# One layer of a hybrid decoder with 32 experts on one core: the scatter of the 64-row tile on quarters of the array, expert weights in 2 MB transfers of 16 KB pieces, waits at every second chunk

## The chip, the cores and the metric

The kernel runs on one core of one Trainium2 chip (trn2). The metric is the device time of one execution in microseconds; lower is better. "PE" in the profile is TensorE, "PEld" its loads of the array's stationary operand, "DVE" VectorE, "ACT" ScalarE, "POOL" GpSimd and "SP" SyncE, which issues all DMAs here.

## What is computed

One step of a decoder layer for 320 tokens (256 of a prompt, 64 of eight short sequences), all in float32: a norm, one input projection, two kinds of recurrent mixers, an output projection, then a mixture of experts, a gated embedding and a last norm. The change is almost wholly in the experts. Their part of the reference, cut:

```python
logits = (xt @ router_w + router_b)                 # 320 x 32
top_val, top_idx = lax.top_k(logits, 4)
gates = jax.nn.softmax(top_val, axis=-1)
# the tokens of each expert in blocks of rows; for each block:
hgu = xb @ w_gu[e] + b_gu[e]                        # w_gu: 32 x 1024 x 2048
gate = jnp.minimum(hgu[:, :D_FF], 7.0)
up = jnp.clip(hgu[:, D_FF:], -7.0, 7.0)
act = (up + 1.0) * gate * jax.nn.sigmoid(1.702 * gate)
y = act @ w_down[e] + b_down[e]                     # w_down: 32 x 1024 x 1024
# gate * y is added to the rows of its tokens
```

## The kernel before

All 32 experts are run, each on a block of up to 64 token slots, and each expert's weights (8 MB for gate and up, 4 MB for down) pass through SBUF once. `ring` is a buffer of 12 slots of 1 MB (8 KB in each of 128 partitions); chunk `c` of an expert stands in slot `c`: eight up chunks (`NGU`), then four down chunks. SyncE loads a chunk with one DMA (L254) as soon as the semaphore `w_used` says that the slot's last reader is through, and the DMA's landing raises `w_full{c}`, on which TensorE waits before the chunk's first matmul. In SyncE's loop (L366 to L376) stand eight waits and loads of gate-up chunks for the next expert and four of down chunks for this one.

TensorE's order is written out by hand in `expert(b, age)` (L1102). A pass of the loop does, for block `b`:

- eight times `up_chunk` (L1074): each chunk has four matmuls, two pairs. A pair uses the two halves of the array's columns: 64 token slots are the stationary operand, the gate columns of the weights stream through the one half and the up columns through the other, 512 columns at a time.
- between them, for block `b - 2`, three times `scatter` (L1064), behind chunks 1, 2 and 3: the expert's result `yS` (64 slots; output columns 0 to 511 in partitions 0 to 63, columns 512 to 1023 in partitions 64 to 127) is multiplied by the transposed selection `SELT`, once for each tile of tokens. Tiles 0 and 1 have 128 tokens, tile 2 has 64. The two matmuls of a scatter use the two halves of the array's rows and write banks 5 and 6 of PSUM. VectorE then adds the banks to `X` (L1976, two adds of 512 columns), and the next scatter waits for that (semaphore `x2`).
- behind chunk 4 `gather(b + 1)` (L1038): the next block's rows are picked out of `XS` by six matmuls; ScalarE copies them to `xrow` (L1362). Behind chunk 6 `turn_rows` (L1046): four transposes of them; ScalarE copies the outcome to `xg` (L1366).
- `turn_select(b - 1)` (L1054): three transposes of the gated selection.
- `down(b - 1)`: four `down_chunk` (L1084), each with four matmuls.
- `turn_hidden(b)` (L1094): eight transposes of the hidden rows `hS`, which ScalarE has copied from PSUM (L1370, L1371). VectorE (L1984 and after) and ScalarE make `act_t` of them, while TensorE goes on.

Which rows of the weights lie in a partition decides which columns must be transposed together. A down chunk holds two neighbouring rows of `w_down` in each partition (`(j p i)`, `i=2`), 8 KB in one piece, and so `turn_hidden` reads every second column of `hS`. Each piece of a gate-up chunk is one row of `w_gu`, 8 KB, and `turn_rows` reads `xrow` column by column:

```python
w_gu = a["expert_w_gu"].rearrange("o e (k p) n -> (o e) p k n", p=P)
w_dn = a["expert_w_down"].rearrange("o e (j p i) n -> (o e) p j (i n)", p=P, i=2)
...
def pair_cols(m):
    return slice(2 * P * (m // 2) + m % 2, 2 * P * (m // 2 + 1), 2)
```

The gate-up bias is transposed once at the start in the same order of columns (L524), sixteen transposes. Blocks 0 and 1 stand ahead of the loop, which runs 30 times; behind it the last down chunks are loaded to slots 0 to 3 and the last sums are made (L1136, L1143), then the gated embedding follows (L1173, L1191).

## Time and profile before

| what | value |
|---|---|
| median of 3 runs | 1428.64 us (1428.08 to 1430.69) |
| profiled execution | 1428.37 us |
| its span, first to last instruction | 1426.6 us |
| TensorE busy | 1343.8 us |
| loads of the array busy | 582.8 us |
| VectorE, ScalarE busy | 503.7, 202.4 us |
| read from HBM | 433.41 MB |
| mean rate over the span | 307 GB/s |
| mean granted clock of TensorE | 0.964 of full speed |

A row of the groups (rows 5 below) gives the line, the engine, what is written and read, the size of the operand, the count, then busy time and mean duration of one, then the idle time ahead of it and what ended it. One matmul of the program appears as two records in the trace, and so does its load; a transpose appears as one. A row of the chain (rows 2, 7 and 8) gives the start, the length and the engine and line that the end of the program hangs on at that time; it follows starts and ends of whole groups, so a piece holds what its group takes including the change to the next.

### The profile page before, as it was taken

How to read it: one execution, taken by the hardware profiler on the slowest of the kernel's cores; microseconds unless marked ns; L12 is line 12 of the kernel's file. 1: busy time of each engine (PE TensorE's matmuls, PEld its weight loads, DVE VectorE, ACT ScalarE, POOL GpSimd, SP SyncE). 2: the span in 40 equal slices, each digit the busy share in tenths (PEclk: the TensorE clock that was granted, in tenths of full speed). 3: DMA queues.
4: the chain of work that ended last, by engine and by line, in shares of the span. 5: the costliest groups of instructions: out<-in, count | busy, mean ns of one | idle time of the engine just before them, and what ended most of it. 6: DMA issues, size and time to landing. Idle time of an engine off the chain costs nothing.

```text
span 1426.6 us, 17293 instructions
## 1 busy us (share of the span) xinstructions
PE 1343.8 (94%) x6116; PEld 582.8 (41%) x6116; DVE 503.7 (35%) x1073; ACT 202.4 (14%) x385; POOL 53.8 (4%) x103
## 2 busy tenths in 40 slices
PE   6989997798669999999999999999999999999997
PEld 5755686573433333333333333333333333333332
DVE  2583344735316233222332223322233222322233
ACT  2450000000111111111111111111111111111111
POOL 5100001000200000000000000000000000000000
PEclk9999999977679999999999999999999999999999
DMA  8231103111459999999999999999999999999931
GB/s 258 68 115 59 59 1 136 58 59 48 120 215 376 421 422 422 422 422 422 422 422 422 422 422 421 422 422 422 420 422 422 422 422 422 422 422 422 422 149 37
DMA packets 83620, 438.82 MB, mean 308 GB/s; under 512 B 15114, under 2 KB 22423, under 8 KB 34410
## 3 DMA queue, kind: packets, MB, share of 16 engines
q1 hardware_dynamic: 83594, 438.47, 75.7%
q8 instruction: 17, 0.28, 0.1%
q14 instruction: 9, 0.07, 0.0%
HBM read 433.41 MB, written 5.02 MB: 307 GB/s over the span
## 4 chain that ended last, share of the span: by engine, by line
PE 89%; DVE 6%; ACT 1%; issue 1%; DMA 1%; SPq 1%; POOLq 0%; POOL 0%; ACTq 0%; DVEq 0%
PE bank L1074 32%; PE bank L1084 16%; PE bank L1064 7%; PE bank L1038 6%; PE bank L576 6%; PE bank L1094 3%; PE bank L1173 2%; PE bank L744 2%; PE bank L574 1%; PE bank L1046 1%; DVE SC L1506 1%; PE bank L1054 1%; PE bank L1014 1%; PE bank L787 1%; DMA SC<-in_ple_w 1%
## 5 line engine op out<-in xcount | busy, mean ns | idle before, releaser
L1074 PE MATMUL bank<-ring,SC 128*64 128x512 f32 x2048 | 479.1, 600 | 0.7 <-ACT SC L1366 0.7
L1074 PEld LDWEIGHTS bank<-ring,SC 128*64 128x64 f32 x2048 | 133.2, 136 | 282.2 <-issue 277.5
L1084 PE MATMUL bank<-ring,SC 128*64 128x512 f32 x1024 | 226.8, 595 | 0.0
L1984 DVE TENSOR_TENSOR SC<-bank,bgu 128x256 f32<-128x256 f32 x128 | 48.1, 418 | 437.1 <-PE bank L1094 437.1
L1976 DVE TENSOR_TENSOR X<-X,bank 128x512 f32<-128x512 f32 x180 | 115.1, 679 | 97.2 <-PE bank L1064 97.2
L1084 PEld LDWEIGHTS bank<-ring,SC 128*64 128x64 f32 x1024 | 70.7, 137 | 133.3 <-issue 133.3
L576 PE MATMUL bank<-xT,ring 128*128 128x320 f32 x384 | 112.5, 442 | 5.8 <-ACTq L1265 4.3
L1064 PE MATMUL bank<-SC 64*128 64x512 f32 x360 | 101.6, 641 | 0.0
L1038 PE MATMUL bank<-XS,SC 128*64 128x512 f32 x396 | 90.6, 592 | 0.7 <-ACT va L1352 0.7
L576 PEld LDWEIGHTS bank<-xT,ring 128*128 128x128 f32 x384 | 71.5, 193 | 36.2 <-ACTq L1265 6.9
L1362 ACT ACTIVATE SC<-bank 128x512 f32<-128x512 f32 x33 | 19.7, 597 | 407.0 <-PE bank L1038 407.0
L1960 DVE TENSOR_SCALAR SC<-iota_s,posb 128x64 f32<-128x64 f32 x99 | 19.1, 250 | 110.5 <-PE bank L1038 110.3
L1064 PEld LDWEIGHTS bank<-SC 64*128 64x128 f32 x360 | 27.1, 184 | 73.0 <-DVE X L1976 48.7
L1038 PEld LDWEIGHTS bank<-XS,SC 128*64 128x64 f32 x396 | 28.4, 137 | 57.5 <-issue 55.9
L431 POOL TENSOR_TENSOR nst<-nst,mhalf 128x1 f32<-128x1 f32 (+2 forms) x10 | 5.6, 573 | 1086.2 <-DVE nst L1456 1080.5
L1094 PEld LDWEIGHTS bank<-ident,SC 128*128 128x128 f32 x256 | 33.1, 208 | 27.2 <-issue 25.2
L1370 ACT ACTIVATE SC<-bank 128x512 f32<-128x512 f32 x32 | 19.1, 597 | 169.3 <-PE bank L1074 169.3
L1379 ACT ACTIVATE SC<-bank 128x512 f32<-128x512 f32 x31 | 18.5, 597 | 171.6 <-PE bank L1084 171.6
L1094 PE MATMUL bank<-ident,SC 128*128 128x128 f32 x256 | 39.2, 296 | 1.2 <-ACT SC L1371 1.2
L744 PE MATMUL bank<-ring,xT 128*128 128x512 f32 x64 | 35.7, 695 | 0.0
L1383 ACT ACTIVATE SC<-SC 128x512 f32<-128x512 f32 x32 | 20.2, 630 | 59.8 <-DVE SC L1992 59.8
L1173 PE MATMUL bank<-ring,xT 128*128 128x512 f32 x64 | 27.9, 594 | 0.0
(463 smaller groups left out, 1048.1 us busy)
## 6 DMA issues: line engine op xcount, KB each, us to landing
ring<-in_expert_w_gu SPq DMA_DIRECT2D x256, 1024.0 KB, 13.8
ring<-in_expert_w_down SPq DMA_DIRECT2D x128, 1024.0 KB, 14.7
ring<-in_w_in SPq DMA_DIRECT2D x7, 2048.0 KB, 8.5
ring<-in_w_out SPq DMA_DIRECT2D x1, 4096.0 KB, 12.8
ring<-in_ple_gate_w SPq DMA_DIRECT2D x4, 1024.0 KB, 10.3
out_gdn_s<-ring SPq DMA_DIRECT2D x1, 2048.0 KB, 10.0
X<-in_x_prompt SPq DMA_DIRECT2D x2, 512.0 KB, 3.9
out_c_s<-ring SPq DMA_DIRECT2D x1, 1024.0 KB, 6.1
```

What stands on the lines that cost most here:

```text
L576: ins = mm(out[:, 0:NTOK], w[:, k, c * P:c * P + P], xT[:, k, :], start=(k == 0), stop=(k == KD - 1))
L744: ins = mm(PB[0][:, :], xT[:, k, OFF[t]:OFF[t] + P], wo[:, k, 512 * n:512 * n + 512], start=(k == 0), stop=(k == KD - 1))
L1038: last = mm(PB[7][SL * h:SL * h + SL, :], SEL[:, t, :], XS[:, t, 512 * h:512 * h + 512], start=(t == 0), stop=(t == 2), skip_group_check=True)
L1064: last = mm(PB[5 + h][:, :], SELT[SL * h:SL * h + SL, P * t:P * t + P], yS[SL * h:SL * h + SL, :], start=True, stop=True)
L1074: last = mm(PB[j][SL * h:SL * h + SL, :], xg[:, c % 4, c // 4, :], w[:, FF * h + 512 * j:FF * h + 512 * j + 512], start=(c == 0), stop=(c ...
L1084: last = mm(PB[4][SL * h:SL * h + SL, :], act_t[:, 2 * (c - NGU) + kk, :], w[:, D * kk + 512 * h:D * kk + 512 * h + 512], start=(c == NGU ...
L1094: last = turn(PB[2 + m // 4][:, P * (m % 4):P * (m % 4) + P], hS[:, pair_cols(m)], ident[:, :])
L1173: last = mm(PB[SUMB[t][n]][0:R, :], xT[:, k, OFF[t]:OFF[t] + R], wple[:, k, 512 * n:512 * n + 512], start=(k == 0), stop=(k == KD - 1))
L1362: A(xrow, PB[7][:, :], ACT.Copy).then_inc(sem("xrow"), 1)
L1383: A(sg, gt, ACT.Sigmoid, scale=ALPHA).then_inc(sem("sig"), 1)
L1976: V.tensor_tensor(dst, dst, PB[5 + h][0:R, :], ALU.add).then_inc(sem("x2"), 1)
L1984: ins = V.tensor_tensor(out[:, 4 * i:4 * i + 4, :], PB[2 + i][:, :].rearrange("p (k h s) -> p k h s", k=4, h=2)[:, :, h, :], bgu[:, c0 + 4 ...
```

## The change

- The weights are loaded two chunks at a time: SyncE's transfers are 2 MB, 16 KB in each partition in one piece. For this, gate-up pairs hold two neighbouring rows of `w_gu` in each partition (`i=2`) and down pairs four of `w_down` (`i=4`). SyncE waits until both chunks of a pair are used, TensorE for `w_full` ahead of every even chunk only.
- With that the transposes read in wider steps: `turn_rows` every second column, `turn_hidden` and the bias at the start every fourth (`spread`).
- Scatter of tile 2: four matmuls instead of two, each on a quarter of the array (64 rows by 64 columns) with 256 columns streamed. VectorE adds them with four adds of 64 x 256.
- The order in `expert`: scatters behind chunks 1, 2 and 4 instead of 1, 2 and 3; the third one's wait on `x2` stands ahead of chunk 4. The gather stands behind chunk 5 (before: 4), `turn_rows` behind chunk 7 (before: 6), directly ahead of `turn_select`.

The diff, cut to its core (the same edit is made at the other loads of SyncE):

```diff
-        w_gu = a["expert_w_gu"].rearrange("o e (k p) n -> (o e) p k n", p=P)
-        w_dn = a["expert_w_down"].rearrange("o e (j p i) n -> (o e) p j (i n)", p=P, i=2)
+        w_gu = a["expert_w_gu"].rearrange("o e (j p i) n -> (o e) p j (i n)", p=P, i=2)
+        w_dn = a["expert_w_down"].rearrange("o e (j p i) n -> (o e) p j (i n)", p=P, i=4)
...
-        def pair_cols(m):
-            return slice(2 * P * (m // 2) + m % 2, 2 * P * (m // 2 + 1), 2)
-
-        def load_chunk(eng, e, c):
-
-            if c < NGU:
-                src, dst = w_gu[e, :, c, :], slot(c)
-            else:
-                src, dst = w_dn[e, :, c - NGU, :], slot(c)
+        def spread(m, n):
+            return slice(n * P * (m // n) + m % n, n * P * (m // n + 1), n)
+
+        def load_pair(eng, e, c):
+
+            dst = ring[:, c * SLOTW:(c + 2) * SLOTW]
+            src = w_gu[e, :, c // 2, :] if c < NGU else w_dn[e, :, (c - NGU) // 2, :]
             eng.dma_start(dst, src).then_inc(sem(f"w_full{c}"), 16)
...
-                for c in range(NGU):
-                    sp.wait_ge(sem("w_used"), used(b, c))
-                    load_chunk(sp, e, c)
+                for c in range(0, NGU, 2):
+                    sp.wait_ge(sem("w_used"), used(b, c + 1))
+                    load_pair(sp, e, c)
...
-                last = turn(PB[2][:, NE * c:NE * c + NE], srow[32:64, pair_cols(c)], ident[32:64, 32:64])
+                last = turn(PB[2][:, NE * c:NE * c + NE], srow[32:64, spread(c, 4)], ident[32:64, 32:64])
...
-                    last = turn(PB[7][:, P * j:P * j + P], xrow[:, P * j:P * j + P], ident[:, :])
+                    last = turn(PB[7][:, P * j:P * j + P], xrow[:, spread(j, 2)], ident[:, :])
...
-                pe.wait_ge(sem("x2"), 6 * b + 2 * t + 1)
-                for h in range(2):
-                    last = mm(PB[5 + h][:, :], SELT[SL * h:SL * h + SL, P * t:P * t + P], yS[SL * h:SL * h + SL, :],
-                              start=True, stop=True)
+                if t < 2:
+                    pe.wait_ge(sem("x2"), 6 * b + 2 * t + 1)
+                for d in range(2 if t == 2 else 1):
+                    for h in range(2):
+                        r = (h + d) % 2
+                        if t < 2:
+                            last = mm(PB[5 + h][:, :], SELT[SL * h:SL * h + SL, P * t:P * t + P], yS[SL * h:SL * h + SL, :],
+                                      start=True, stop=True)
+                        else:
+                            last = mm(PB[5 + h][64 * r:64 * r + 64, 0:256], SELT[SL * h:SL * h + SL, 256:320],
+                                      yS[SL * h:SL * h + SL, 256 * r:256 * r + 256], start=True, stop=True, skip_group_check=True)
...
-                pe.wait_ge(sem(f"w_full{c}"), 16 * b + 16)
+                if c % 2 == 0:
+                    pe.wait_ge(sem(f"w_full{c}"), 16 * b + 16)
...
-                pe.wait_ge(sem(f"w_full{at}"), 16 * b + (16 if at == c else 32))
+                if c % 2 == 0:
+                    pe.wait_ge(sem(f"w_full{at}"), 16 * b + (16 if at == c else 32))
...
-                    last = turn(PB[2 + m // 4][:, P * (m % 4):P * (m % 4) + P], hS[:, pair_cols(m)], ident[:, :])
+                    last = turn(PB[2 + m // 4][:, P * (m % 4):P * (m % 4) + P], hS[:, spread(m, 4)], ident[:, :])
...
                 for c in range(NGU):
+                    if age >= 2 and c == 4:
+                        pe.wait_ge(sem("x2"), 6 * (b - 2) + 5)
                     up_chunk(b, c)
...
-                    if age >= 2 and 1 <= c <= 3:
-                        scatter(b - 2, c - 1)
-                    if c == 4:
+                    if age >= 2 and c in (1, 2, 4):
+                        scatter(b - 2, c // 2 if c > 1 else 0)
+                    if c == 5:
                         gather(b + 1)
-                    if c == 6:
+                    if c == 7:
                         turn_rows(b + 1)
...
                 for h in range(2):
-                    dst = X[0:R, t, 512 * h:512 * h + 512]
-                    V.tensor_tensor(dst, dst, PB[5 + h][0:R, :], ALU.add).then_inc(sem("x2"), 1)
+                    if t < 2:
+                        dst = X[0:R, t, 512 * h:512 * h + 512]
+                        ins = V.tensor_tensor(dst, dst, PB[5 + h][0:R, :], ALU.add)
+                    else:
+                        for r in range(2):
+                            dst = X[0:64, 2, 512 * h + 256 * r:512 * h + 256 * r + 256]
+                            ins = V.tensor_tensor(dst, dst, PB[5 + h][64 * r:64 * r + 64, 0:256], ALU.add)
+                    ins.then_inc(sem("x2"), 1)
```

TensorE's order in the loop, from behind the second scatter to the down matmuls, before. `bank` is PSUM, `ring` the weights, `SC` the expert's small tiles; "x4" are four matmuls of a chunk, and a `REGISTER_ALU` works out the value of a wait:

```order
L1064 MATMUL bank<-SC 128x512 x2
L1074 MATMUL bank<-ring,SC 64x512 x4
L1062 REGISTER_ALU
L1064 MATMUL bank<-SC 128x512 x2
L1074 MATMUL bank<-ring,SC 64x512 x4
L1035 REGISTER_ALU
L1038 MATMUL bank<-XS,SC 64x512 x6
L1074 MATMUL bank<-ring,SC 64x512 x8
L1046 MATMUL bank<-ident,SC 128x128 x4
L1074 MATMUL bank<-ring,SC 64x512 x4
L1054 MATMUL bank<-ident,SC 128x128 x3
```

The same stretch of TensorE's loop in the changed kernel (its lines: L1065 and L1068 scatter, L1079 up, L1035 gather, L1043 rows, L1051 selection):

```order
L1065 MATMUL bank<-SC 128x512 x2
L1079 MATMUL bank<-ring,SC 64x512 x4
L1112 REGISTER_ALU
L1079 MATMUL bank<-ring,SC 64x512 x4
L1068 MATMUL bank<-SC 64x256 x4
L1079 MATMUL bank<-ring,SC 64x512 x4
L1032 REGISTER_ALU
L1035 MATMUL bank<-XS,SC 64x512 x6
L1079 MATMUL bank<-ring,SC 64x512 x8
L1043 MATMUL bank<-ident,SC 128x128 x4
L1051 MATMUL bank<-ident,SC 128x128 x3
```

The third scatter has moved one chunk on and has four matmuls of 64x256 in place of two of 128x512; the gather has moved one chunk on; the four and the three transposes stand side by side.

SyncE's loads of down chunks in its loop, before:

```order
L372 ISA
L372 TENSOR_LOAD etab
L372 ISA x2
L374 REGISTER_ALU
L254 ISA
L254 DMA ring<-in_expert_w_down 128x2048
L374 REGISTER_ALU
L254 ISA
L254 DMA ring<-in_expert_w_down 128x2048
L374 REGISTER_ALU
L254 ISA
L254 DMA ring<-in_expert_w_down 128x2048
```

and the same place in the changed kernel:

```order
L370 ISA
L370 TENSOR_LOAD etab
L370 ISA x2
L372 REGISTER_ALU
L252 ISA
L252 DMA ring<-in_expert_w_down 128x4096
L372 REGISTER_ALU
L252 ISA
L252 DMA ring<-in_expert_w_down 128x4096
```

Two transfers of 4096 numbers a partition stand where four of 2048 stood (the fourth is not shown); the gate-up loads ahead of them go from eight to four in the same way.

## Rows read from the trace of the kernel before

**Rows 1.** The page: TensorE's busy time, its tenths in 40 slices, the chain's shares

```profile
PE 1343.8 (94%) x6116; PEld 582.8 (41%) x6116; DVE 503.7 (35%) x1073; ACT 202.4 (14%) x385; POOL 53.8 (4%) x103
...
PE   6989997798669999999999999999999999999997
...
PE 89%; DVE 6%; ACT 1%; issue 1%; DMA 1%; SPq 1%; POOLq 0%; POOL 0%; ACTq 0%; DVEq 0%
```

**Rows 2.** The chain in one pass of the expert loop (start us, us, what)

```profile
701.23 7.02 PE bank L1084 x32
708.25 1.16 PE bank L1094 x8
...
712.99 1.06 PE bank L1064 x4
714.05 1.87 PE bank L1074 x8
...
724.34 3.43 PE bank L1074 x16
727.77 0.59 PE bank L1046 x4
728.36 1.87 PE bank L1074 x8
730.23 0.48 PE bank L1054 x3
730.71 7.02 PE bank L1084 x32
```

**Rows 3.** Windows: us, PE PEld DVE ACT POOL busy, granted clock, DMA share, GB/s

```profile
53.00:58.00 5.00, 5.00 (x20) 3.56 (x19) 2.79 (x6) 3.00 (x8) 0.00 (x0) 1.00 1.03 391
...
236.00:245.00 9.00, 4.03 (x33) 3.51 (x31) 8.21 (x23) 0.94 (x3) 1.05 (x1) 0.83 1.02 405
...
701.23:730.71 29.48, 29.48 (x137) 9.89 (x139) 8.77 (x20) 3.79 (x8) 0.00 (x0) 1.00 1.01 422
```

The first window has input weights in pieces of 2 KB on the way, the second output weights in pieces of 4 KB, the third the expert weights in pieces of 8 KB.

**Rows 4.** SyncE's chunk loads (L254): issue to landing of all, then of the last

```profile
DMA to landing us min/median/max: 4.7/14.1/20.8
...
L254 SPq DMA_DIRECT2D ring<-in_expert_w_down x1: 333/333/333, 1327.4 to 1327.4; - x1
...
DMA to landing us min/median/max: 20.8/20.8/20.8
```

**Rows 5.** Loads of the array by line and shape, whole execution

```profile
L1094 PEld LDWEIGHTS bank<-ident,SC 128*128 128x128 f32 x256 | 33.1, 208 | 27.2 <-issue 25.2 <-ACT SC L1371 2.1
...
L1064 PEld LDWEIGHTS bank<-SC 64*128 64x128 f32 x360 | 27.1, 184 | 73.0 <-DVE X L1976 48.7 <-issue 24.3
L1046 PEld LDWEIGHTS bank<-ident,SC 128*128 128x128 f32 x132 | 13.8, 140 | 27.5 <-issue 26.0 <-ACT SC L1362 1.6
...
L1054 PEld LDWEIGHTS bank<-ident,SC 128*128 128x128 f32 x96 | 9.9, 140 | 25.9 <-issue 25.9
```

**Rows 6.** Timeline at the second scatter (start us, us, engine, line, idle before)

```profile
714.15 1.28 DVE L1976 TENSOR_TENSOR X<-X,bank 128x512 f32<-128x512 f32 x2
...
715.84 0.30 PEld L1064 LDWEIGHTS bank<-SC 64*128 64x128 f32 x4 [0.81 <-DVE X L1976]
...
717.02 1.28 DVE L1976 TENSOR_TENSOR X<-X,bank 128x512 f32<-128x512 f32 x2 [1.60 <-PE bank L1064]
```

**Rows 7.** The chain at the start: the transposes of the gate-up bias

```profile
13.88 1.53 PE bank L524 x13
15.42 1.90 PE bank L538 x8
```

**Rows 8.** The chain behind the expert loop

```profile
1356.73 1.16 PE bank L1094 x8
1357.89 1.06 PE bank L1136 x4
...
1367.17 7.04 PE bank L1084 x32
1374.21 0.02 issue
```

More of the change, by code:

```diff
@@ L317, in _ @@
             sp.wait_ge(sem("rows_stored"), 32)
-            for c in range(0, 2):
-                load_chunk(sp, 0, c)
+            for c in range(0, 2, 2):
+                load_pair(sp, 0, c)
             sp.wait_ge(sem("Sp_done"), 2)
@@ L329, in _ @@
             sp.wait_ge(sem("wqST_ps"), 1)
-            for c in range(2, 4):
-                load_chunk(sp, 0, c)
+            for c in range(2, 4, 2):
+                load_pair(sp, 0, c)
             sp.wait_ge(sem("Ss_done"), H)
@@ L335, in _ @@
             sp.wait_ge(sem("S_stored"), 16)
-            for c in range(4, 6):
-                load_chunk(sp, 0, c)
+            for c in range(4, 6, 2):
+                load_pair(sp, 0, c)
             sp.wait_ge(sem("qC_ps"), 2)
@@ L349, in _ @@
             sp.wait_ge(sem("C_stored"), 32)
-            for c in range(6, 8):
-                load_chunk(sp, 0, c)
+            for c in range(6, 8, 2):
+                load_pair(sp, 0, c)
             sp.wait_ge(sem("mnew"), 3)
@@ L355, in _ @@
             sp.wait_ge(sem("x1_ps"), 5)
-            for c in range(NGU, NCK):
-                load_chunk(sp, 0, c)
+            for c in range(NGU, NCK, 2):
+                load_pair(sp, 0, c)
             sp.wait_ge(sem("lg_ps"), 3)
             sp.dma_start(bdr, a["expert_b_down"].rearrange("o e n -> (o e) n")).then_inc(sem("bdr_in"), 16)
-            for c in range(NGU):
-                sp.wait_ge(sem("w_used"), used(0, c))
-                load_chunk(sp, 1, c)
+            for c in range(0, NGU, 2):
+                sp.wait_ge(sem("w_used"), used(0, c + 1))
+                load_pair(sp, 1, c)
             sp.wait_ge(sem("routed"), ROUTED["tables"])
```

15 lines of the change are left out of this document (7 added, 8 removed).

## The prediction

> **What bounds the kernel now.** I read the page's busy shares and slices first, then the chain of waits over one pass of the expert loop, then the loads of the array, then the transfers.
>
> TensorE is busy 94% of the span and the chain is 89% TensorE; from a third of the span on its slices are full [rows 1]. In the expert loop it has no gap: one pass, from one group of down matmuls (L1084) to the next, runs 701.23 to 730.71 = 29.48 us, and every piece of the chain in it is a PE piece [rows 2]. 384 up and down chunks of 1 MB pass in 32 experts. So TensorE sets the pace, and what the change does to its instructions decides, unless the transfers come to bind.
>
> They are near. The same pass brings 12 chunks, 12.58 MB; at 422 GB/s with the 16 engines' time full [rows 3] that is 29.8 us, slightly more than TensorE's 29.48. It costs nothing yet: the time from issue to landing only grows, from 4.7 us at first to 20.8 us at the last chunk [rows 4], while a slot is needed again 29.48 - 1.7 = 27.8 us after its release. A faster TensorE uses this reserve up.
>
> **The change, part by part.**
>
> *Waits at every second chunk: 0.* Two chunks without a change of tile take 3.43 us, one of them after a change takes 1.87 us [rows 2]. A chunk is 1.72 us, four steps of 0.43, and nothing is left over for its wait. The registers and waits run ahead.
>
> *Scatter of the 64-row tile on quarters: -12.9 us.* A scatter takes 1.06 us [rows 2]: two steps of 0.53, each with both halves side by side (four records, L1064), 0.43 of streaming 512 columns and 0.10 around it. The third now has four matmuls of 64x64 with 256 columns. All four at once give 2 x (0.215 + 0.10) = 0.63, 0.43 less; two after two give 1.06, no gain. Halves of rows and halves of columns each run side by side here (L1064, L1074), so I take 0.43. It runs 30 times (360 loads, 12 a pass [rows 5]): 30 x 0.43 = 12.9. The entry and exit are the same as before. The scatter moves past a chunk, and its wait on VectorE's adds stands a chunk earlier, before chunk 4: the second tile's adds start with the scatter behind chunk 2 and there is all of chunk 3 between, 1.7 us for adds of 1.28 [rows 6]. VectorE's four adds of 256 columns instead of two of 512 are on an engine with 8.77 of 29.48 us busy [rows 3]; if that cover were gone, two more instructions could cost at most what the pair takes now, 1.28 us a pass. The earlier two scatters keep their one chunk of distance and their small margin (the adds end at 715.43, the next scatter starts at 715.84 [rows 6]).
>
> *Transposes of the gathered rows moved behind chunk 7, next to those of the selection: -6.5 us.* Four transposes take 0.59 and three 0.48 [rows 2], so 0.11 each and 0.15 fixed. In one run the second 0.15 goes, and so does the 0.155 by which the chunk between them is longer than 1.715: 0.31. Against it, the four now read every second column. The eight L1094 transposes, which do that already, take 1.16 where 0.15 + 8 x 0.11 = 1.03 would be expected; for four I take 0.10. Net 0.21 x 31 passes = 6.5, and 0.2 back for the two unmerged runs. ScalarE's copies that follow have the 7.02 us of the down matmuls [rows 2] as cover. The gather also moves one chunk; it keeps two chunks, 3.43 us, ahead of its transposes, and no one waits.
>
> *Transposes of the hidden rows at every fourth column: +25.6 us, the term that decides.* Nothing in the profile loads the array at a step of four. A load at step one takes 140 ns (L1046, L1054), one at step two 208 (L1094) [rows 5]: 68 more, of which only some 15 reach the step from transpose to transpose (0.11 to 0.125), since the load lies behind the transpose ahead. That cover is now used up. Bounds: nothing more, if only "not contiguous" counts; below nothing is excluded, as no row shows a wider step loading faster than a narrow one. Above: the same 68 ns again, or 136 if it goes by the stretch of memory read, which doubles. All of it is uncovered then: 8 x 0.068 = 0.54 to 8 x 0.136 = 1.09 us a pass. I take 0.80, between these two, since the one step that the rows show (one to two) did cost: the step becomes 0.22. 32 x 0.80 = 25.6.
>
> The Trainium skill, "Advanced Engine Details and Errata", section Memory Cachelines, says that accesses run at full speed while they hit the same 16-byte line, that two hits on a line are needed, and that a different line per access pays. Every second float has two hits, every fourth has one: by the rule the old step would be free and the new one not. The trace disagrees with the first half (208 against 140 ns); no run here shows the second. By the rule alone the term is there but unpriced; without it, it could be 0.
>
> *The same at the start: +1.6.* Sixteen transposes (L524) go from every second column to every fourth, on the chain [rows 7]: 16 x 0.10.
>
> *2 MB transfers of 16 KB pieces: 0 on the path.* The rate rises with the piece: 391 GB/s at 2 KB, 405 at 4 KB, 422 at 8 KB [rows 3]. Half of the last step again, 2%, gives 430, and 12.58 MB take 29.3 us; bounds 422 (29.8) and 439 (28.7). The Trainium skill, "DMA: Bandwidth & Descriptors", section Where 436 GB/s comes from, has a ceiling of 435 GB/s, an estimate of 28.9 us by it. SyncE issues six transfers instead of twelve, each only when both chunks are used, and TensorE waits for the whole pair: the reserve shrinks by about 1.7 + 2.5 = 4.2 us. With TensorE at 29.48 - 0.43 - 0.21 + 0.80 = 29.64 us a pass the transfers are faster than it, and this stays cover.
>
> **Sum:** -12.9 - 6.5 + 0.2 + 25.6 + 1.6 = +8.0 us. The profiled execution took 1428.37 (its span is 1426.6), so 1436.4; the median of the three runs is 0.3 higher, and I say **1436.5 us**. A change of 0.2%, 2.9 us, is about the least that a measurement of this kernel can tell from none.
>
> **The rivals.**
>
> *The wide step is free and the transfers keep up (22%).* Then -12.9 - 6.5 + 0.2: 1409.2. For it: L1094's step of transposes lengthened by 15 ns only, and a fixed slow rate for anything not contiguous fits the rows as well. TensorE would need 28.84 us a pass, transfers 29.3 at 430 GB/s; the lag of 0.46 x 30 = 14 us on a first 7.2 reaches 21, under the 28.84 - 3.43 = 25.4 that a pair has. Against it: the single comparison the rows allow went up.
>
> *It is free and the transfers bind (8%).* If 16 KB pieces run at 422 GB/s as 8 KB ones do, the queue is never empty and its last load for expert 30 lands as now, 1327.4 + 20.8 = 1348.2 [rows 4]. Behind it TensorE has two chunks, 3.43, the transposes, 1.16, and 1357.89 to 1374.21, 16.3 [rows 8]: 1369.1, against 1374.21. So 5.1 us are won at most: 1423.3. For it: the full share of the engines; against it: the rate has risen with every doubling of the piece.
>
> *The quarters don't run side by side (8% with a free step).* -6.5 + 0.2 = 1422.1; with the forecast's step 1449. Nothing in the loop uses both halves of rows and of columns at once. This is the change not doing what its name says.
>
> *The wide step costs less than 68 ns (15%).* With a step from 0.17 to 0.19 the sum is within 2.9 us of nothing (10%); below 0.17 it is 1416 to 1425 (5%). The sum turns positive where eight transposes lengthen by some 0.57 us, a step of 0.19.
>
> *Waiting for pairs stalls TensorE at the start.* Expert 1's chunks land 4.7 us after issue and have most of a pass; no chance of its own.
>
> **How the numbers follow.** My forecast (the step is 0.19 or more) has 47%, all of it slower by over 0.2%; its own range is 1430 to 1447, from the bounds of 0.54 and 1.09 with the quarters at work. Faster: 22 + 8 + 8 + 5 = 43%. Same: 10%. The range of 1408 to 1445 takes in all the faster cases down to 1409 with 1 us for the rate, and leaves out the top of the forecast's own range and the sum in which the quarters fail too, together with what falls below less than 20%. Both signs are likely here; they are apart because one unmeasured duration of 0.1 us occurs 256 times.
>
> **What would show it.** The pass of the loop by the chain: 29.6 us, against 28.8 with a free step and 29.3 with binding transfers. Loads of the hidden rows' transposes above 270 ns and their eight in about 1.95 us, against 208 and 1.16. The third scatter at 0.63, against 1.06. Seven transposes in a run at about 1.0. Load rate in the loop near 430 GB/s where it is saturated; with a pass of 29.6 it sits below, at 425, and landing times stay flat, under 12 us. A wait of TensorE on ring loads would speak for binding transfers. I am wrong if the eight transposes take under 1.5 us, and wrong in the mechanism if TensorE shows idle time on transfers.

## The result and the profile after

| what | before | changed |
|---|---|---|
| median | 1428.36 us (1427.00 to 1430.69, 4 runs) | 1412.91 us (1410.66 to 1413.97, 4 runs) |
| ratio of the two, 95% interval | | 0.9888 (0.9870 to 0.9906) |
| profiled execution, its span | 1428.37, 1426.6 us | 1413.97, 1412.2 us |
| TensorE busy | 1343.8 us | 1328.6 us |
| loads of the array busy | 582.8 us | 589.8 us |
| VectorE busy | 503.7 us | 515.7 us |

The change is faster by 1.1%, 15.5 us. The forecast was 1436.5 us, slower by 8. The result lies inside the range of 1408 to 1445, but on the other side of the kernel before. It is nearest to a case that the prediction gave 22%: 1409.2 for a wide step that costs nothing.

The page of the changed kernel, the same rows as [rows 1], with the rate of each slice and the two leading lines of the chain:

```profile
PE 1328.6 (94%) x6236; PEld 589.8 (42%) x6236; DVE 515.7 (37%) x1133; ACT 202.5 (14%) x385; POOL 53.9 (4%) x103
...
PE   6989997798859999999999999999999999999997
...
GB/s 260 65 119 60 60 1 124 71 60 0 162 224 291 428 429 427 429 429 428 427 429 428 428 429 428 428 428 429 428 428 429 428 428 428 428 429 428 428 184 37
...
PE 75%; DMA 15%; DVE 6%; issue 2%; ACT 2%; SPq 1%; POOLq 0%; POOL 0%; ACTq 0%; DVEq 0%
PE bank L1079 27%; DMA ring<-in_expert_w_gu 14%; PE bank L1090 12%; PE bank L573 6%; PE bank L1035 5%; PE bank L1065 4%; PE bank L1100 2%; PE bank L1181 2%; PE bank L741 2%; PE bank L571 1%; DVE SC L1514 1%; PE bank L1043 1%; PE bank L784 1%; DMA SC<-in_ple_w 1%; PE bank L1068 1%
```

Before, TensorE had 89% of the chain and DMAs 1%. Now loads of gate-up weights have 14% of it. The busy shares don't show this: TensorE is as full as it was. The 14% is no price: in the last passes the chain can be followed through the transfers or through TensorE, and half_bytes below puts what the transfers cost at 4.4 us.

The chain in one early pass of the changed kernel, which answers to [rows 2] (L1079 up, L1065 and L1068 scatter, L1035 gather, L1043 rows, L1051 selection, L1090 down, L1100 hidden rows):

```profile
703.74 1.16 PE bank L1100 x8
704.91 3.58 PE bank L1079 x16
708.49 1.06 PE bank L1065 x4
709.55 1.87 PE bank L1079 x8
711.42 1.06 PE bank L1065 x4
712.48 3.58 PE bank L1079 x16
716.06 0.59 PE bank L1068 x8
716.65 1.87 PE bank L1079 x8
718.52 2.58 PE bank L1035 x12
721.10 3.43 PE bank L1079 x16
724.53 0.67 PE bank L1043 x4
725.20 0.33 PE bank L1051 x3
725.53 7.02 PE bank L1090 x32
732.55 1.17 PE bank L1100 x8
```

The pass takes 732.55 - 703.74 = 28.81 us, 0.67 less than before. The third scatter takes 0.59 instead of 1.06. The seven transposes stand in one run of 1.00, and the chunks around the moved pieces are no longer split. The eight transposes at every fourth column take 1.16, which is what they took at every second.

The loads of the array, as [rows 5]:

```profile
L1100 PEld LDWEIGHTS bank<-ident,SC 128*128 128x128 f32 x256 | 33.4, 211 | 25.9 <-issue 25.1 <-ACT SC L1379 0.7
L1043 PEld LDWEIGHTS bank<-ident,SC 128*128 128x128 f32 x132 | 18.3, 207 | 27.5 <-issue 26.0 <-ACT SC L1370 1.6
...
L1068 PEld LDWEIGHTS bank<-SC 64*64 64x64 f32 x240 | 6.2, 131 | 24.3 <-issue 24.3
```

L1100 (before: L1094) went from a step of two to one of four and from 208 to 211 ns. L1043 (before: L1046) went from consecutive columns to every second and from 140 to 207.

An early and a late pass as windows, with the columns of [rows 3]:

```profile
703.74:732.55 28.81, 28.81 (x141) 10.00 (x140) 9.15 (x22) 3.79 (x7) 0.00 (x0) 1.00 1.01 429
1147.84:1177.20 29.36, 29.09 (x141) 9.99 (x142) 9.15 (x22) 3.79 (x7) 0.00 (x0) 1.00 1.01 429
```

The chain around the end of that late pass, and of the one before it:

```profile
1118.48 24.27 DMA ring<-in_expert_w_gu
...
1142.80 1.94 PE bank L1079 x8
1144.74 1.06 PE bank L1065 x4
...
1147.84 24.28 DMA ring<-in_expert_w_gu
```

TensorE's waits for gate-up weights (us in total, times, longest):

```profile
PEld bank L1079 <- DMA ring<-in_expert_w_gu: 9.4, 10, 1.0
```

From issue to landing of the 2 MB loads of SyncE (L252), whole execution, as [rows 4]:

```profile
DMA to landing us min/median/max: 7.6/20.1/25.5
```

From one expert's first chunk to the next one's, 21 passes take 28.81 us, one 29.26 and the last seven 29.36. 12.58 MB at 428.5 GB/s are 29.36 us: the late passes go at the pace of the transfers. The pair of chunks 2 and 3 is released, its load lands 24.3 us later, and TensorE is there already. The landing times of all pairs grow to 25.5 us at most and stay there. That is the 28.81 - 3.43 = 25.4 us that a pair has; the pair in the chain above has a scatter between its chunks and so only some 24. TensorE's short waits recur in every late pass (ten for gate-up weights, the longest 1.0 us, and ten for down weights, 4.7 us together). Their sum is not the loss: ahead of chunk 2 the loads of the array stand idle for 0.76 us in the early pass too, where no transfer is late, and for 0.96 us in the late one.

**Where the 14.4 us of span came from.** Up to the start of expert 0: +1.8 (429.24 against 427.43). From there to the end of the last down matmuls: 1359.88 - 429.24 = 930.64 against 1374.21 - 427.43 = 946.78, so -16.1. Behind it: 52.3 against 52.4. Across the twelve profiles below, the start of expert 0 lies between 425.6 and 432.5 us. In the chain there it hangs on the landing of one load of the gated embedding (`ple_w`), beside which expert loads and stores are under way: 13.7 us after its issue before, 13.1 in the changed kernel, 15.1 in pairs_only and changed_again. This spread of several us lies ahead of all that is argued over, so I compare the **stretch** from expert 0's first matmul to the last expert's first one: 900.9 us before, 884.9 after.

### The profile page after: what moved, and what is told of

Its sections match the earlier page's. It is cut to its first block, busy times and chain, and to the rows that moved or that the text cites. A ratio compares the mean times of both kernels' runs of the same rounds, so it can differ in the third digit from the quotient of the medians.

```text
span 1412.2 us, 16885 instructions
## 1 busy us (share of the span) xinstructions
PE 1328.6 (94%) x6236; PEld 589.8 (42%) x6236; DVE 515.7 (37%) x1133; ACT 202.5 (14%) x385; POOL 53.9 (4%) x103
## 4 chain that ended last, share of the span: by engine, by line
PE 75%; DMA 15%; DVE 6%; issue 2%; ACT 2%; SPq 1%; POOLq 0%; POOL 0%; ACTq 0%; DVEq 0%
PE bank L1079 27%; DMA ring<-in_expert_w_gu 14%; PE bank L1090 12%; PE bank L573 6%; PE bank L1035 5%; PE bank L1065 4%; PE bank L1100 2%; PE bank L1181 2%; PE bank L741 2%; PE bank L571 1%; DVE SC L1514 1%; PE bank L1043 1%; PE bank L784 1%; DMA SC<-in_ple_w 1%; PE bank L1068 1%
## 5 line engine op out<-in xcount | busy, mean ns | idle before, releaser
L1079 PE MATMUL bank<-ring,SC 128*64 128x512 f32 x2048 | 474.0, 599 | 3.0 <-ACT SC L1374 0.7
L1079 PEld LDWEIGHTS bank<-ring,SC 128*64 128x64 f32 x2048 | 136.0, 136 | 288.8 <-issue 257.4
L1090 PE MATMUL bank<-ring,SC 128*64 128x512 f32 x1024 | 226.8, 595 | 0.0
L1090 PEld LDWEIGHTS bank<-ring,SC 128*64 128x64 f32 x1024 | 70.6, 137 | 133.3 <-issue 127.8
L1985 DVE TENSOR_TENSOR X<-X,bank 128x512 f32<-128x512 f32 x120 | 76.8, 681 | 49.8 <-PE bank L1065 49.8
L1035 PE MATMUL bank<-XS,SC 128*64 128x512 f32 x396 | 90.6, 592 | 0.7 <-ACT va L1360 0.7
L1989 DVE TENSOR_TENSOR X<-X,bank 64x256 f32<-64x256 f32 x120 | 50.1, 418 | 92.2 <-PE bank L1068 90.5
L1065 PE MATMUL bank<-SC 64*128 64x512 f32 x240 | 67.7, 641 | 0.0
L1035 PEld LDWEIGHTS bank<-XS,SC 128*64 128x64 f32 x396 | 28.4, 137 | 57.5 <-issue 56.0
L1100 PEld LDWEIGHTS bank<-ident,SC 128*128 128x128 f32 x256 | 33.4, 211 | 25.9 <-issue 25.1
L1100 PE MATMUL bank<-ident,SC 128*128 128x128 f32 x256 | 39.5, 297 | 0.5 <-ACT SC L1379 0.5
L1065 PEld LDWEIGHTS bank<-SC 64*128 64x128 f32 x240 | 18.1, 184 | 48.7 <-issue 24.3
L741 PE MATMUL bank<-ring,xT 128*128 128x512 f32 x64 | 36.8, 713 | 0.0
L1043 PEld LDWEIGHTS bank<-ident,SC 128*128 128x128 f32 x132 | 18.3, 207 | 27.5 <-issue 26.0
## 6 DMA issues: line engine op xcount, KB each, us to landing
ring<-in_expert_w_down SPq DMA_DIRECT2D x64, 2048.0 KB, 20.8
ring<-in_w_out SPq DMA_DIRECT2D x1, 4096.0 KB, 12.9
```

Of the source, the lines that this page charges most:

```text
L741: ins = mm(PB[0][:, :], xT[:, k, OFF[t]:OFF[t] + P], wo[:, k, 512 * n:512 * n + 512], start=(k == 0), stop=(k == KD - 1))
L1035: last = mm(PB[7][SL * h:SL * h + SL, :], SEL[:, t, :], XS[:, t, 512 * h:512 * h + 512], start=(t == 0), stop=(t == 2), skip_group_check=True)
L1043: last = turn(PB[7][:, P * j:P * j + P], xrow[:, spread(j, 2)], ident[:, :])
L1065: last = mm(PB[5 + h][:, :], SELT[SL * h:SL * h + SL, P * t:P * t + P], yS[SL * h:SL * h + SL, :], start=True, stop=True)
L1079: last = mm(PB[j][SL * h:SL * h + SL, :], xg[:, c % 4, c // 4, :], w[:, FF * h + 512 * j:FF * h + 512 * j + 512], start=(c == 0), stop=(c ...
L1090: last = mm(PB[4][SL * h:SL * h + SL, :], act_t[:, 2 * (c - NGU) + kk, :], w[:, D * kk + 512 * h:D * kk + 512 * h + 512], start=(c == NGU ...
```

## The experiments

The theory: an operand that isn't read consecutively costs one fixed amount, whatever the step; TensorE then needs 28.81 us a pass; the reserve in landing times is used up after some 22 passes, and from there the transfers set the pace at 29.36 us. The rivals are named A to J in the expectations. The edits are cut to their core.

| kernel | median, us | of the kernel before (95%) | pass, early and late, us | stretch, us |
|---|---|---|---|---|
| before | 1427.65 to 1431.04 | 1 | 29.48 | 900.9 |
| quarters_only | 1424.96 | 0.9966 (0.9953 to 0.9979) | 29.01, 29.82 | 895.7 |
| order_only | 1424.30 | 0.9963 (0.9949 to 0.9976) | 29.17, 29.82 | 896.0 |
| no_quarters | 1423.95 | 0.9953 (0.9940 to 0.9966) | 29.27, 29.27 | 894.1 |
| pairs_only | 1433.04 | 1.0015 (1.0003 to 1.0027) | 29.57, 29.57 | 903.7 |
| changed_again | 1414.87 | 0.9892 (0.9870 to 0.9913) | 28.81, 29.37 | 885.0 |
| early_half | 1416.44 | 0.9903 (0.9882 to 0.9925) | 28.81, 29.37 | 886.2 |
| half_bytes | 1409.29 | 0.9856 (0.9832 to 0.9880) | 28.81, 28.81 | 880.5 |
| pieces_8k | 1428.12 | 0.9980 (0.9965 to 0.9994) | 28.71, 29.82 | 898.5 |
| hidden_step1 | 1410.18, one run | | 28.67, 29.36 | 884.8 |
| hidden_step8 | 1412.31, one run | | 28.73, 29.36 | 883.9 |
| q_rowmajor | 1413.12, one run | | 28.81, 29.37 | 884.1 |
| early_half_again | 1409.88, one run | | 28.81, 29.36 | 884.3 |

The first four shared their runs of the kernel before (median 1429.71), and so did the next four (1431.04) and the last four (1427.65, one run).

### quarters_only: the scatter on quarters alone

The kernel before, with the new `scatter`, its adds, and its place; nothing else.

```diff
+                    if age >= 2 and c == 4:
+                        pe.wait_ge(sem("x2"), 6 * (b - 2) + 5)
...
-                    if age >= 2 and 1 <= c <= 3:
-                        scatter(b - 2, c - 1)
+                    if age >= 2 and c in (1, 2, 4):
+                        scatter(b - 2, c // 2 if c > 1 else 0)
```

> The kernel before with one part of the change: the scatter of tile 2 on quarters with its four adds, behind chunk 4 and with its wait ahead of that chunk. Loads of 1 MB, the transposes and their places stay as before. Theory (TensorE sets the pace until the reserve of landing time is used up, then the transfers of 8 KB pieces at 422 GB/s, 29.82 us for an expert): a pass of 29.475 - 0.47 = 29.0 us at first and of 29.82 once the landing time reaches its end, TensorE then waits for ring loads; the last load lands at the same time as before, 1348 us, and the kernel gains only 5 to 9 us of the 14 that thirty quarters' scatters are worth: 1419 to 1423 us. Rival A (the transfers never bind at 8 KB pieces, the late passes of the changed kernel have another cause): 29.0 us in all passes, 1414.5 us. Rival B (the quarters gain nothing by themselves, the gain came from the order or from the pairs): no difference, 1428 us.

Measured: 0.34% faster, 4.8 us by the medians, 5.3 in the stretch. The early passes take 29.01 us. After 18 of them in the loop come one of 29.21 and ten of 29.82. An early and a late pass as windows:

```profile
710.00:739.01 29.01, 29.01 (x141) 9.79 (x141) 9.16 (x23) 3.79 (x7) 0.00 (x0) 1.00 1.02 423
1177.00:1206.82 29.82, 29.46 (x141) 9.57 (x139) 9.25 (x23) 3.78 (x7) 0.00 (x0) 1.00 1.01 422
```

The waits for weights, and then the landing times:

```profile
PEld bank L1091 <- DMA ring<-in_expert_w_down: 20.2, 25, 1.2
PEld bank L1081 <- DMA ring<-in_expert_w_gu: 18.4, 23, 0.9
```

```profile
DMA to landing us min/median/max: 4.7/22.2/27.4
```

The quarters save 0.47 us a pass, and of the 29 x 0.47 = 13.6 us in the stretch some three fifths are lost again to transfers in 8 KB pieces. The kernel before had 6 us left in landing times (20.8 against some 27) and no more. The third scatter takes 0.59 us in its chain. Rivals A and B fall.

### order_only: the new order alone

```diff
-                    if c == 4:
+                    if c == 5:
                         gather(b + 1)
-                    if c == 6:
+                    if c == 7:
                         turn_rows(b + 1)
```

The scatters stand behind chunks 1, 2 and 4, with the old two matmuls.

> The kernel before with only the new order of TensorE: scatters behind chunks 1, 2 and 4, the gather behind chunk 5, the four transposes of the gathered rows behind chunk 7 beside the three of the selection, still column by column. Theory (a run of transposes has a fixed part that is saved once, and the chunks beside it are not split): the pass is 0.31 us shorter, 29.17 us, until the transfers bind at 29.82 us; 1419 to 1421 us. Rival C (merging is worth little, the fixed part is paid at each change of what is read): 29.4 us, 1426 us. Rival A, with no bound by transfers: 1419 us.

Measured: 0.37% faster, 4.9 us in the stretch; passes of 29.17, then 29.82. The size of a pass was right, 0.31 less, but the 1419 to 1421 us expected for the whole were too low. The late passes, seven of 29.82 and one of 29.5, give back 4.9 us, and I had set that too small. There is one gain that neither forecast nor expectation had: the two passes ahead of the loop together take 45.05 us instead of 46.09. In expert 0 TensorE has nothing to do between its last up chunk and the hidden rows but to wait for ScalarE's copies. The chain there, in quarters_only (the old place of the row transposes, L1046) and then in order_only:

```profile
443.59 0.59 PE bank L1046 x4
444.18 1.89 PE bank L1081 x8
...
446.09 0.60 ACT SC L1379
446.69 0.50 ACT SC L1380
```

```profile
440.99 3.46 PE bank L1074 x16
...
444.47 0.60 ACT SC L1370
445.07 0.50 ACT SC L1371
```

Behind chunk 7 the four transposes fall into that wait of 1.10 us and vanish from the chain.

### no_quarters: everything but the quarters

The changed kernel, with the old two matmuls of 512 columns for tile 2 and its two adds.

```diff
-                for d in range(2 if t == 2 else 1):
-                    for h in range(2):
...
+                for h in range(2):
+                    last = mm(PB[5 + h][:, :], SELT[SL * h:SL * h + SL, P * t:P * t + P], yS[SL * h:SL * h + SL, :],
+                              start=True, stop=True)
```

> The changed kernel with the old two matmuls of 512 columns for tile 2, at their new place. Theory: the third scatter goes from 0.59 back to 1.06 us, the pass from 28.81 to 29.27 us, just inside what transfers of 16 KB pieces allow (29.36 us an expert), so TensorE never waits for them and the late passes are 29.27 as well; the kernel is 7 to 9 us slower than the changed one: 1420 to 1422 us. That is less than the 14 us of thirty scatters, because the changed kernel's last eight passes take 29.36 us. Rival B (quarters gain nothing): 1413 us. Rival A (the transfers don't bind in the changed kernel): the whole 14 us, 1427 us.

Measured: the third scatter at 1.06 us again, all passes 29.27, landing times at most 18.0 us, and not one wait on ring loads. It is slower than the changed kernel by 9.1 us in the stretch (894.1 against 885.0), where 29 passes of 0.46 would make 13.3. The expectation had this, 7 to 9.

### pairs_only: the transfers alone

The kernel before with 2 MB loads, halved waits and the wider steps, in the old order and with the old scatter.

```diff
-                    last = turn(PB[2 + m // 4][:, P * (m % 4):P * (m % 4) + P], hS[:, pair_cols(m)], ident[:, :])
+                    last = turn(PB[2 + m // 4][:, P * (m % 4):P * (m % 4) + P], hS[:, spread(m, 4)], ident[:, :])
```

> The kernel before with only the transfers changed: 2 MB in 16 KB pieces, waits at every second chunk, and the wider steps of the transposes that go with them (rows every second column, hidden rows and bias every fourth). Scatter and order as before. Theory (a step of four costs the same as a step of two; a step of two instead of one costs the four transposes of rows 0.1 us in a pass): the pass is 29.58 us against 29.48, 28 to 29 transfers' worth of slack at 29.36, so 1429 to 1432 us, slightly slower than before. Rival D (the wide step of the hidden rows costs and something else in the changed kernel paid for it): eight transposes over 1.3 us, 1435 us or more. Rival E (the pairs are a gain of their own, by fewer waits or better bandwidth): under 1426 us.

Measured: passes of 29.57 us, 0.10 more than before; 2.8 us more in the stretch, slower by 0.15% (0.03 to 0.27). The four row transposes at a step of two take 0.67 us instead of 0.59, 0.08 of the 0.10. The hidden rows' eight at a step of four take what they took:

```profile
711.50 1.16 PE bank L1093 x8
...
731.03 0.67 PE bank L1043 x4
```

Rivals D and E fall. By themselves, the large transfers are a small loss. They pay because the other two parts need them (pieces_8k below).

### changed_again: the changed kernel beside the next three

> The changed kernel once more, beside the next three on the same chip, so that they can be compared with it directly. 15 us below the kernel before (ratio 0.9888 as first measured), loop passes of 28.81 us for the first 22 and 29.36 for the last seven or eight.

Measured: 0.9892 (0.9870 to 0.9913), 28.81 and 29.37 us a pass, a stretch of 885.0 us. The stretch repeats within 0.2 us while the whole time of this profile is 3.5 us above that of the first, 3.3 of it ahead of expert 0 (432.54 against 429.24).

### half_bytes: TensorE without the bound

```diff
+            if e is not 0:
+                dst = ring[:, c * SLOTW:(c + 1) * SLOTW]
+                src = w_gu[e, :, c // 2, 0:SLOTW] if c < NGU else w_dn[e, :, (c - NGU) // 2, 0:SLOTW]
+                eng.dma_start(dst, src).then_inc(sem(f"w_full{c}"), 16)
+                return
```

> The changed kernel, in whose loop and last loads only the first half of each pair (1 MB of the 2 MB) is loaded for every expert but the first, while all matmuls are kept; so half of the weights that are multiplied are those of expert 0. Theory (TensorE alone would hold 28.81 us, the late 29.36 are the transfers'): all passes 28.81 us, 0.55 x 8 = 4.4 us less than the changed kernel, and landing times that stay at 3 to 8 us. Rival A (the late passes come from something else that grows, a queue or the clock): still 29.36 at the end, same time as the changed kernel. Rival F (TensorE itself is slowed by the transfers into its buffer): passes shorter than 28.81 throughout, by more than 0.1 us.

From expert 1 on this kernel leaves out half of each pair of weights. The two very last loads stayed whole, unlike what the expectation says. A middle and a late pass as windows, and then the landing times of the halved loads (L253):

```profile
700.00:728.81 28.81, 28.81 (x141) 9.99 (x139) 9.15 (x22) 3.78 (x7) 0.00 (x0) 1.00 0.66 218
1147.84:1176.65 28.81, 28.81 (x141) 9.99 (x139) 9.15 (x22) 3.78 (x7) 0.00 (x0) 1.00 0.65 218
```

```profile
DMA to landing us min/median/max: 4.9/5.1/5.4
```

All passes take 28.81 us, and the stretch is 880.5: 4.4 us less than in the changed kernel. That is the whole price of the late passes, and it is the transfers' (rival A falls). Half the traffic (218 GB/s for 429) doesn't make TensorE's early passes shorter by a hundredth: the transfers slow it only by coming late (rival F falls).

### pieces_8k: the piece or the transfer

2 MB transfers as before, but each of two 8 KB pieces a partition.

```diff
+            dst = ring[:, c * SLOTW:(c + 2) * SLOTW].rearrange("p (k n) -> p k n", k=2)
+            src = w_gu[e, :, c:c + 2, :] if c < NGU else w_dn[e, :, c - NGU:c - NGU + 2, :]
```

> The changed kernel with transfers of 2 MB made of two 8 KB pieces a partition instead of one of 16 KB; the transposes go back to the steps of the kernel before (rows column by column, hidden rows every second column). Theory (the rate goes by the size of the piece, 422 GB/s at 8 KB against 428.5 at 16 KB, and not by the size of the transfer or the number of issues): 29.82 us an expert once the reserve is used, early passes 28.7, the kernel 8 to 11 us slower than the changed one, 5 to 7 us faster than the one before. Rival G (the rate goes by the size of the transfer or the number of DMAs): 29.36 us late passes, and the kernel as fast as the changed one or 1 to 3 us faster, since its four transposes of rows are cheaper.

Measured: 13.3 us slower than the changed kernel by the medians (1428.12 against 1414.87) and 13.4 in the stretch, more than the 8 to 11 expected; 0.2% faster than before. An early and a late pass as windows:

```profile
703.00:731.71 28.71, 28.71 (x141) 9.89 (x139) 9.16 (x22) 3.78 (x7) 0.00 (x0) 1.00 1.01 422
1148.00:1177.82 29.82, 29.19 (x140) 9.80 (x140) 9.25 (x22) 3.78 (x7) 0.00 (x0) 1.00 1.01 422
```

With transfers of 2 MB and pieces of 8 KB the rate is the 422 GB/s of the kernel before, so it goes by the piece, not by the size or the number of transfers (rival G falls). The size of the loss shows how such an end is worked out: both kernels are bound by their transfers at the end, so the difference is that of the streams over the whole loop, 29 x (29.82 - 29.36) = 13.3 us, and not the excess over TensorE's pace in some passes. Beside quarters_only (895.7), which has the same stream but waits and loads chunk by chunk, it is 2.8 us later, although its TensorE is faster. Its landing times end at 26.0 us against 27.4, and its first load lands 7.6 us after its issue against 4.7: larger transfers start later and leave less reserve. That this is all of the 2.8 is argued, not shown.

### hidden_step1 and hidden_step8: the term of the forecast

```diff
-                    last = turn(PB[2 + m // 4][:, P * (m % 4):P * (m % 4) + P], hS[:, spread(m, 4)], ident[:, :])
+                    last = turn(PB[2 + m // 4][:, P * (m % 4):P * (m % 4) + P], hS[:, P * m:P * m + P], ident[:, :])
```

(`spread(m, 8)` in the second.) Both multiply the hidden columns by other rows of `w_down` than they belong to; the number and the shapes of all operations stay the same.

> The changed kernel with the eight transposes of the hidden rows reading consecutive columns instead of every fourth. It changes the computation: the rows of the down projection are multiplied in another order. Theory (a load that isn't contiguous costs a fixed amount more, a contiguous one 140 ns): loads of 140 ns, eight transposes in 1.00 to 1.05 us instead of 1.16, early passes 28.68 us, late ones still 29.36, the same end within 1 us. Rival H (what costs is the place, ScalarE's copy just before, not the step): loads stay at 208 ns or more and the eight at 1.16.

> The changed kernel with the eight transposes of the hidden rows reading every eighth column; the computation changes in the same way. Theory: a load of 208 to 215 ns as at steps two and four, eight transposes in 1.16 us, passes of 28.81. Rival I (the load grows with the step, but four is still under the first threshold): loads over 270 ns, the eight above 1.5 us. With 140 at step one, 208 at two and 211 at four this run tells whether the forecast's term exists at any step.

Measured, for step one: the group of loads, and the eight transposes in the chain.

```profile
L1100 PEld LDWEIGHTS bank<-ident,SC 128*128 128x128 f32 x256 | 27.4, 140 | 25.9 <-issue 25.1 <-ACT SC L1379 0.7
```

```profile
727.48 1.02 PE bank L1100 x8
```

The same two for step eight:

```profile
L1100 PEld LDWEIGHTS bank<-ident,SC 128*128 128x128 f32 x256 | 31.0, 194 | 25.8 <-issue 25.1 <-ACT SC L1379 0.7
```

```profile
702.50 1.09 PE bank L1100 x8
```

So 140, 208, 211 and 194 ns at steps of one, two, four and eight, and 1.02, 1.16, 1.16 and 1.09 us for the eight. A step that isn't one costs 54 to 71 ns a load, of which 9 to 18 ns reach the next transpose, and up to eight a wider step costs no more than a step of two; eight is even the cheapest of the three. Rivals H and I fall. The early passes follow to the hundredth (28.67, 28.81, 28.73). The stretches hardly do: the transfers take back what step one gains.

### q_rowmajor: the order of the four quarters

```diff
-                for d in range(2 if t == 2 else 1):
-                    for h in range(2):
-                        r = (h + d) % 2
+                for h in range(2):
+                    for d in range(2 if t == 2 else 1):
+                        r = d
```

> The changed kernel with the four matmuls of the third scatter in another order: the two that share a half of the rows follow each other, instead of alternating between the halves. Theory (four quarters run at once, in whatever order they are issued): 0.59 us for the four as before, all starts within 30 ns. Rival J (two matmuls that share rows of the array go one after the other unless others stand between): the four take 0.8 to 1.06 us, and the pass 29.0 to 29.3.

Measured, the third scatter in the chain:

```profile
716.01 0.59 PE bank L1068 x8
```

0.59 us, as before, and the first records of the four matmuls start within 20 ns in both kernels. Rival J falls: the four quarters take the same time whichever are neighbours in the order.

### early_half, twice: a start for the stream

```diff
-            for c in range(0, NGU, 2):
+            for c in range(2):
+                sp.wait_ge(sem("w_used"), used(0, c))
+                sp.dma_start(slot(c), w_gu[1, :, 0, SLOTW * c:SLOTW * c + SLOTW]).then_inc(sem(f"w_full{c}"), 16)
+            for c in range(2, NGU, 2):
```

Not shown: TensorE waits for `w_full1` ahead of chunk 1 of expert 1.

> The changed kernel, with the very first pair that is loaded while the experts run (expert 1, chunks 0 and 1) split into two loads of 1 MB, the first of them issued when chunk 0 is used instead of when both are. Theory (the transfers run without a pause from there to the last load, and at the end TensorE goes at their pace, so what the stream starts earlier the end comes earlier): the last load lands 1.6 to 1.7 us earlier, the late passes of 29.36 us start about three passes later, the kernel is 1.5 us faster than the changed one. Rival A (the late passes aren't set by the transfers): no difference. This is also the one cheap step past both kernels.

> The kernel with the first pair of expert 1 in two loads once more. In its first profile the stream did start 1.7 us earlier after the start of expert 0, but lost more than that 24 to 29 us in, where packets took 0.7 to 1.4 us instead of 0.61. If that is a chance event of the memory, this profile doesn't show it, the last load lands 917.5 to 918 us after the start of expert 0 (919.1 and 919.3 in the two profiles of the changed kernel, 920.5 in the first of this one), and the late passes start at the 24th or later. If it belongs to the kernel, the same slow stretch and 920.5 come again.

The first gave no gain (1416.44 against 1414.87 for the changed kernel, stretch 886.2 against 885.0), and the second little: 884.3, where unchanged streams lie between 884.1 and 885.0 (q_rowmajor, changed_again). Windows of the ten us from 20 us after the start of expert 0, in early_half, its repeat and changed_again:

```profile
450.45:460.45 10.00, 10.00 (x50) 3.43 (x48) 4.04 (x11) 0.71 (x2) 0.00 (x0) 1.00 0.93 357
```

```profile
445.69:455.69 10.00, 10.00 (x50) 3.43 (x48) 4.05 (x11) 0.71 (x2) 0.00 (x0) 1.00 0.94 378
```

```profile
452.54:462.54 10.00, 10.00 (x50) 3.43 (x48) 4.05 (x11) 0.71 (x2) 0.00 (x0) 1.00 1.00 424
```

The second half of the pair did land 0.7 to 1.4 us earlier after the start of expert 0 than the whole pair in the two profiles of the changed kernel, but both profiles lost 0.5 to 0.7 MB in this stretch, more than 1 us of transfer. So the slow stretch is not an accident of one profile. It doesn't belong to this edit either: the same ten us moved 347 GB/s in quarters_only, 388 in order_only and 373 in pairs_only, but 422 to 435 in the other profiles that have the new order and load the pairs whole. Why it happens stays open. In the repeat the last load landed 918.5 us after the start of expert 0, between the two cases of its expectation, where unchanged streams (q_rowmajor, changed_again) land at 918.3 and 919.3. Its late passes began with the 23rd loop pass, as in q_rowmajor, and not with the 24th. How much an earlier start is worth is therefore not shown. What the first profile and changed_again do show is the tie at the end: there the last load landed 1.2 us later (920.4 against 919.2), and the last expert began 1.2 us later. No version that computes the whole layer was found to beat the changed kernel by more than its own profiles differ.

## Why the prediction was wrong

- **The step that failed:** "*Transposes of the hidden rows at every fourth column: +25.6 us, the term that decides*", 32 x 0.80, a step from transpose to transpose of 0.22 us. It measured 0: 1.16 us for the eight at steps of two and of four, and loads of 208 and 211 ns. The forecast took the one step that the rows showed (140 to 208 ns from one to two) for the first on a slope. hidden_step8 shows that it is a plateau, at least up to eight. It also let all of a further rise fall on the path, on the ground that the cover was used up; no load here took longer than 211 ns, so no run tests that.
- The Trainium skill, "Advanced Engine Details and Errata", section Memory Cachelines, speaks of two hits on a 16-byte line that are needed for full speed. By the rule the step of two floats, with two hits, would run like consecutive columns, and four and eight, with one, would be slower. The rows put the break between one and two (140, 208) and none between two and four (208, 211). For loads of the array in float32 the measurement decides, against the rule at both places.
- **Bias at the start, +1.6:** 0. Its group of 13 takes 1.53 us, as in [rows 7]. The same error.
- **The chances around that step** don't follow from the sum either. By the prediction's own terms the whole comes to nothing at a step of about 0.20 us, not 0.19, and at 0.17 it is some 7 us faster, not within 2.9. The lower bound of 0.54 us gives about 1428, not 1430, so not all of the forecast's case was slower by over 0.2%.
- **Scatter on quarters, -12.9:** right, and a little small. 1.06 to 0.59 us, so 0.47 instead of 0.43; 30 x 0.47 = 14.1. The four start together, and the part around the streaming is 0.08 a step instead of the 0.10 assumed.
- **Transposes in one run, -6.5 + 0.2:** right in the loop, 29.48 - 28.81 - 0.47 = 0.20 against 0.21, with the 0.10 for a step of two near what pairs_only shows (0.08 to 0.10). Wrong ahead of the loop: -0.94 instead of +0.2, since expert 0's four transposes slip into a wait for ScalarE.
- **Adds of VectorE, waits at every second chunk:** 0, as said. The four adds take 1.73 us instead of 1.28 and nobody waits for them.
- **Transfers of 16 KB pieces, 0 on the path:** the rate was right, 428.5 GB/s for 430, 29.36 us an expert for 29.3. The "0" hung on the slow pass of 29.64 and fell with it. The first rival counted on this: a lag of 0.46 a pass on a first 7.2 us would reach 21 of the 25.4 us. The lag was 0.55 a pass (half_bytes: 28.81 against 29.36), and it began at 12.0 to 13.5 us, not 7.2, because the loads queue behind each other already during expert 0. The landing times of the two down pairs in the first loop pass, 12.0 for the first and 13.5 for the second:

```profile
L252 SPq DMA_DIRECT2D ring<-in_expert_w_down x2: 332/334/337, 470.0 to 473.5; - x2
DMA to landing us min/median/max: 12.0/12.7/13.5
```

  The second is the one that reaches the end of its reserve: (25.4 - 13.5) / 0.55 = 21.6, so the reserve was bound to run out after 21 or 22 passes, and 21 passes took 28.81 us. The eight behind them cost 4.4 us. The second rival's sum (5.1 us won at most where transfers stay at 422 GB/s) was about right for pieces of 8 KB: by the medians quarters_only won 4.8 us, order_only 5.4 and pieces_8k 2.9.

The sum with measured terms, for the stretch (29 loop passes): 29 x 0.67 = 19.4, 0.9 ahead of the loop, together -20.4 (half_bytes: 900.9 - 880.5 = 20.4), and 4.4 given back to the transfers: -16.0, the measured 900.9 - 884.9.

The parts don't add up one by one: in the stretch, the quarters alone gave -5.3, the order alone -4.9, the transfers alone +2.8, together -7.4, while the change gave -16.0. Each of the first two ran into the transfers in 8 KB pieces at 29.82 us, and the third, which is slower by itself, raised that bound.

## What to carry to other kernels

- Before pricing an unmeasured access pattern by extrapolation, ask whether the measured points are a slope or a step. Two points fit both; a term that rests on them and occurs 256 times deserves both values as cases of nearly equal weight.
- A kernel with two streams near balance ends with the slower one. Work out the end of the transfers as well (start + number x time each, less the reserve in landing time) and take the later of the two; landing times that grow from pass to pass are this reserve being spent, while the busy shares still look like TensorE alone.
- Parts of a change that look useless alone can carry the others. Undoing one part of the changed kernel tells more than trying one part on the old one.

## What the runs showed of the hardware

- A load of the array of 128x128 float32 takes 140 ns from consecutive columns, 208, 211 and 194 ns at every second, fourth and eighth. Of the extra 54 to 71 ns, 9 to 18 reach the distance between transposes.
- Four float32 matmuls of 64x64 with 256 columns on the four quarters of the array have their first records start within 20 ns, in either of two orders, and take 0.59 us with what lies around them, where two of 64x128 with 512 columns on the halves of the rows take 1.06.
- Loads from HBM, with one core at work, ran at 422 GB/s in pieces of 8 KB, in transfers of 1 MB and of 2 MB alike, and at 428.5 in pieces of 16 KB, in transfers of 2 MB. The Trainium skill, "DMA: Bandwidth & Descriptors", section Where 436 GB/s comes from, has a ceiling of 435 GB/s for the ports of SBUF, and these rates stay under it. It also says that between HBM and SBUF the HBM side binds, at about 358 for a core, half of what two cores have together. The one core at work here went beyond that, and the measurement decides.
- A matmul pass of 28.81 us was the same to a hundredth with 429 and with 218 GB/s running into the buffer that it read.
